# Stick-breaking attention: suffix sums on VectorE's scan instead of matmuls, and another order inside the banded-attention steps

## The reference, cut to what matters

```python
# banded: 4 key/value heads, 8 query heads each, chunks of 64 queries, keys: 16 meta + 3 chunks
m = max(max(sc), sink); e = exp(sc - m); p = e / (sum(e) + exp(sink - m))
# stick-breaking, per head of 128 columns, blocks of 128 queries
z = einsum('bhqd,bhkd->bhqk', q_blk, k) * scale
causal = key_pos[None, :] < q_pos[:, None]
log_keep = where(causal, log_sigmoid(-z), 0.0)
suffix = cumsum(log_keep, axis=3, reverse=True) - log_keep
a = where(causal, exp(log_sigmoid(z) + suffix), 0.0)
out = einsum('bhqk,bhkd->bhqd', a, v)
```

## Time and profile before

| | |
|---|---|
| median of 3 runs | 2866.44 us (2866.18 to 2867.0) |
| the profiled execution, its time | 2866.59 us |
| its span | 2864.8 us |
| PE busy | 2824.8 us (99%) |
| PE weight loads busy | 2442.3 us (85%) |
| DVE busy | 1244.1 us (43%) |
| ACT busy | 976.8 us (34%) |
| POOL busy | 1166.4 us (41%) |
| mean DMA | 86 GB/s |

### The profile page before, as it was taken

How to read it: one execution, slowest core, us unless ns; L and a number is a source line. 1 busy time by engine, 2 the same in 40 slices (tenths; PEclk the granted TensorE clock), 3 DMA queues, 4 the chain that set the end, 5 groups by cost and what they waited for, 6 DMA issues and landing times.

```text
span 2864.8 us, 41154 instructions
## 1 busy us (share of the span) xinstructions
PE 2824.8 (99%) x16928; PEld 2442.3 (85%) x16928; DVE 1244.1 (43%) x2202; ACT 976.8 (34%) x1433; POOL 1166.4 (41%) x888
## 2 busy tenths in 40 slices
PE   8999999999999999999999999999999999999997
PEld 8999999999999999777877778878778787787775
DVE  6333333433343358353434352723323244455646
ACT  4323222222323244344233344532323333234442
POOL 4333433334333435333434337434344343445442
PEclk9999999999999999999999999999999999999998
DMA  4122222222222212222222234222222222222222
GB/s 184 70 89 74 89 75 74 79 85 74 86 77 75 88 69 89 89 74 74 89 74 75 88 110 148 89 74 89 87 76 88 86 77 76 101 81 89 89 89 74
DMA packets 37084, 247.68 MB, mean 86 GB/s; under 512 B 3985, under 2 KB 4130, under 8 KB 8354
## 3 DMA queue, kind: packets, MB, share of 16 engines
q1 hardware_dynamic: 35728, 241.36, 23.7%
q10 hardware_dynamic: 1170, 3.70, 0.4%
HBM read 240.85 MB, written 4.19 MB: 86 GB/s over the span
## 4 chain that ended last, share of the span: by engine, by line
PE 90%; DVE 4%; ACT 2%; DMA 1%; DVEq 1%; POOL 1%; issue 0%; ACTq 0%; SPq 0%
PE pj L301 20%; PE pj L307 20%; PE pj L305 20%; PE pj L362 3%; PE pj L366 3%; PE pj L364 3%; PE pj L1138 2%; PE pj L1140 2%; PE pj L1139 2%; PE pa L508 1%; PE pa L545 1%; POOL wl L2273 1%; PE pa L1069 1%; DMA raw<-in_stream 1%; PE pa L1493 1%; PE pa L1475 1%
## 5 line engine op out<-in xcount | busy, mean ns | idle before, releaser
L2273 POOL TENSOR_TENSOR wl<-raw,wh 128x512 fp32r<-128x512 f32 x884 | 1166.2, 1351 | 1663.1 <-ACT wh L273 1663.0
L301 PE MATMUL pj<-xh,wh 128*128 128x264 f32 (+2 forms) x3728 | 1079.9, 336 | 3.5 <-POOL wl L2273 2.3
L307 PE MATMUL pj<-xh,wl 128*128 128x264 f32 (+2 forms) x3728 | 1047.4, 327 | 0.0
L305 PE MATMUL pj<-xl,wh 128*128 128x264 f32 (+2 forms) x3728 | 1045.6, 327 | 0.0
L273 ACT ACTIVATE wh<-raw 128x2048 fp32r<-128x2048 f32 x221 | 423.1, 1914 | 972.0 <-PE pj L307 620.7
L301 PEld LDWEIGHTS pj<-xh,wh 128*128 128x128 f32 x3728 | 632.4, 189 | 76.9 <-issue 19.8
L305 PEld LDWEIGHTS pj<-xl,wh 128*128 128x128 f32 x3728 | 631.3, 188 | 59.9 <-issue 5.3
L307 PEld LDWEIGHTS pj<-xh,wl 128*128 128x128 f32 x3728 | 631.3, 188 | 59.6
L388 DVE TENSOR_TENSOR acc<-pj,acc 128x528 f32<-128x528 f32 (+1 forms) x192 | 134.2, 700 | 126.7 <-PE pj L366 125.6
L362 PE MATMUL pj<-oh,wh 128*128 128x264 f32 (+1 forms) x640 | 180.1, 330 | 2.4 <-DVE acc L388 1.3
L366 PE MATMUL pj<-oh,wl 128*128 128x264 f32 (+1 forms) x640 | 177.7, 326 | 0.0
(11 more groups left out here) (317 smaller groups left out, 2726.9 us busy)
## 6 DMA issues: line engine op xcount, KB each, us to landing
raw<-in_stream SPq DMA_DIRECT2D x221, 1024.0 KB, 4.8
acc<-in_x SPq DMA_DIRECT2D x8, 528.0 KB, 10.1
out_y<-acc SPq DMA_DIRECT2D x8, 512.0 KB, 2.9
arena<-in_mem ACTq DMA_DIRECT2D x2, 1024.0 KB, 6.6
cst<-in_cst SPq DMA_DIRECT2D x1, 448.0 KB, 13.4
cos<-in_cos_a SPq DMA_DIRECT2D x1, 264.0 KB, 13.5
sin<-in_sin_a SPq DMA_DIRECT2D x1, 264.0 KB, 13.7
cos<-in_cos_b ACTq DMA_DIRECT2D x1, 264.0 KB, 2.6
```

What stands on the lines that cost most here:

```text
L301: pe.matmul(pj[:, pu, b, 0:m], whk, xh[:, k, a:a + m], start=(k == 0), stop=False)
L305: pe.matmul(pj[:, pu, b, 0:m], whk, xl[:, k, a:a + m], start=False, stop=False)
L307: ins = pe.matmul(pj[:, pu, b, 0:m], wlk, xh[:, k, a:a + m], start=False, stop=(k == KD - 1))
L2273: pool.tensor_tensor(wl[:, j, at], raw[:, j, at], wh[:, j, at].bitcast(F32), ALU.subtract).then_inc(s_part if c < LO_PARTS - 1 else s_lo, 1)
```

## The change

In the stick-breaking heads z is formed with queries on the partitions, in blocks of 128, 256, 384 and 512 columns (the operands of `sb_z` change places). DVE adds a large negative number above the diagonal (`mask`, four operations on PSUM). The three ACT passes stay. DVE adds max(z, 0), runs four `tensor_tensor_scan` operations over the reversed columns, one for each block, and subtracts the result from z in one operation. ACT takes the exponential; PE transposes ten 128x128 blocks of it (`sb_tr`, after `s_ae`) in place of the seven matmuls of `sb_c`; ACT copies them to SBUF (`S_eT`, the space of `S_sp`), and `sb_pv` reads that. The hook of `sb_c` at tile 2 step 12 (tile 5 step 12) goes; `sb_tr` stands at tile 3 step 2 (tile 6 step 2), `sb_pv` at tile 3 step 11 (before 10) and tile 6 step 9 (before 5), and the sums of squares one step later and four steps later.

In the banded attention each slot on PE does the scores first, then the product, then the transposes. DVE takes the maxima first, then copies the product, normalises, and only then runs `meanwhile`. ACT runs the sigmoid of a tile behind the tile's first slot, not ahead of it.

Three constant matrices go (`strict`, `neg_low`, `neg_ones`), and `cst` shrinks from 7 to 4 blocks of 128 columns.

```diff
@@ b_slot (PE): the block of chunk i is moved, unchanged, ahead of those of i-2 and i-1
+                c, n = i, B_CH * g + i
+                if c < B_CH:
+                    if n >= 1:
+                        pe.wait_ge(s_bexp, n)
+                    if c == 0:
+                        pe.wait_ge(s_bsk, g + 1)
+                        pe.wait_ge(s_bq, 4 * g + 4)
+                    at, lo, w = b_band(c)
...
                 c, n = i - 2, B_CH * g + i - 2
@@ b_slot_dve
-            c, n = i - 2, B_CH * g + i - 2
-            if 0 <= c < B_CH:
-                dve.wait_ge(s_bpv, n + 1)
-                dve.tensor_copy(B_qc[:, c, :], (bank1, bank3)[c % 2][:, 0:2 * P]).then_inc(s_bo, 1)
             c, n = i, B_CH * g + i
...
                 dve.tensor_scalar(B_nb, B_mx, -B_scale, None, ALU.mult).then_inc(s_bnb, 1)
-            if meanwhile is not None:
-                meanwhile()
+            c, n = i - 2, B_CH * g + i - 2
+            if 0 <= c < B_CH:
+                dve.wait_ge(s_bpv, n + 1)
+                dve.tensor_copy(B_qc[:, c, :], (bank1, bank3)[c % 2][:, 0:2 * P]).then_inc(s_bo, 1)
...
                 dve.sem_inc(s_bnorm, 1)
+            if meanwhile is not None:
+                meanwhile()
@@ b_act
-                if m > 0:
-                    sigmoid(act, O_B0 + 4 * g + m, SEQ)
-                for i, k in enumerate(B_POS[g]):
-                    if KD * m <= k < KD * (m + 1):
-                        b_slot_act(act, g, i)
+                slots = [i for i, k in enumerate(B_POS[g]) if KD * m <= k < KD * (m + 1)]
+                for i in slots:
+                    b_slot_act(act, g, i)
+                    if m > 0 and i == slots[0]:
+                        sigmoid(act, O_B0 + 4 * g + m, SEQ)
@@ sb_z
-                for i in (0, 1, 3, 2):
-                    w = SEQ - P * i
-                    ins = pe.matmul(pa[:, S_off[i]:S_off[i] + w], S_k[:, P * i:P * (i + 1)], S_q[:, P * i:SEQ],
-                                    start=(i != 3), stop=False, skip_group_check=True)
+                for i in range(NQ):
+                    w = P * (i + 1)
+                    ins = pe.matmul(pa[:, S_zoff[i]:S_zoff[i] + w], S_q[:, P * i:P * (i + 1)], S_k[:, 0:w],
+                                    start=True, stop=True, skip_group_check=True)
@@ sb_c -> sb_tr
-                pe.wait_ge(s_sp, n + 1)
+                pe.wait_ge(s_ae, n + 1)
                 for i in range(NQ):
-                    w = SEQ - P * i
-                    ins = pe.matmul(pa[:, S_off[i]:S_off[i] + w], neg_low, S_sp[:, S_off[i]:S_off[i] + w],
-                                    start=False, stop=(i == NQ - 1), skip_group_check=True)
-                    if i < NQ - 1:
-
-                        ins = pe.matmul(pa[:, S_off[i] + P:S_off[i] + w], neg_ones, S_behind[i], start=False,
-                                        stop=True, skip_group_check=True)
-                ins.then_inc(s_c, 1)
+                    for kb in range(i + 1):
+                        at = S_off[kb] + P * (i - kb)
+                        ins = pe.transpose(pa[:, at:at + P], S_e[:, S_zoff[i] + P * kb:S_zoff[i] + P * (kb + 1)], ident)
+                ins.then_inc(s_tr, 1)
@@ sb_pe
-            hooks = {1: {8: [sb_z(n)]}, 2: {6: [sb_vt(n)], 12: [sb_c(n)]}, 3: {10: [sb_pv(n, n)]},
-                     4: {2: [head_ss_pe(n, S_sq)], 8: [sb_z(n + 1)]}, 5: {6: [sb_vt(n + 1)], 12: [sb_c(n + 1)]},
-                     6: {5: [sb_pv(n + 1, n + 1)], 10: [head_ss_pe(n + 1, S_sq)]}}
+            hooks = {1: {8: [sb_z(n)]}, 2: {6: [sb_vt(n)]}, 3: {2: [sb_tr(n)], 11: [sb_pv(n, n)]},
+                     4: {3: [head_ss_pe(n, S_sq)], 8: [sb_z(n + 1)]}, 5: {6: [sb_vt(n + 1)]},
+                     6: {2: [sb_tr(n + 1)], 9: [sb_pv(n + 1, n + 1)], 14: [head_ss_pe(n + 1, S_sq)]}}
@@ sb_act
-                    act.wait_ge(s_z, n + a + 1)
+                    act.wait_ge(s_zm, n + a + 1)
...
+                if j in (3, 6):
+                    act.wait_ge(s_tr, n + a + 1)
+                    act.activation(S_eT, pa[:, 0:S_ZW], ACT.Copy).then_inc(s_a, 1)
@@ sb_dve: softplus and the old weights give way to
+            def mask(n):
+                dve.wait_ge(s_z, n + 1)
+                for i in range(NQ):
+                    d = pa[:, S_zoff[i] + P * i:S_zoff[i] + P * (i + 1)]
+                    dve.scalar_tensor_tensor(d, tri, NEG, d, ALU.mult, ALU.add)
+                dve.drain()
+                dve.sem_inc(s_zm, 1)
+
+            def weights(n):
                 dve.wait_ge(s_l, n + 1)
                 dve.scalar_tensor_tensor(S_sp, pa[:, 0:S_ZW], 0.0, S_e, ALU.max, ALU.add)
                 dve.drain()
                 for i in range(NQ):
...
+                    x = S_sp[:, S_zoff[i]:S_zoff[i] + P * (i + 1)][:, ::-1]
+                    dve.tensor_tensor_scan(x, x, x, 0.0, ALU.add, ALU.max)
                 dve.drain()
...
+                dve.scalar_tensor_tensor(S_e, S_sp, -1.0, pa[:, 0:S_ZW], ALU.mult, ALU.add).then_inc(s_am, 1)
```

More of the change, by code:

```diff
@@ L114, in build @@
         o_in_x = (xsh[:, KD - 2:KD, :], xsl[:, KD - 2:KD, :])
-        cst = sb("cst", 7 * P)
-        ident, ones, tri, strict, neg_low, neg_ones, tri64 = (cst[:, i * P:(i + 1) * P] for i in range(7))
+        cst = sb("cst", 4 * P)
+        ident, ones, tri, tri64 = (cst[:, i * P:(i + 1) * P] for i in range(4))
         par = sb("par", NPAR)
@@ L209, in build @@
         s_l = sem("s_l")
-        s_sp = sem("s_sp")
-        s_c = sem("s_c")
+        s_zm = sem("s_zm")
+        s_tr = sem("s_tr")
         s_am = sem("s_am")
@@ L1032, in f @@
             def f(pe):
+                c, n = i, B_CH * g + i
[6 more added lines that the diff above has]
+                    at, lo, w = b_band(c)
+                    for mp in range(2):
+                        for a in range(2):
+                            h = slice(64 * a, 64 * a + 64)
+                            ins = pe.matmul(B_sc[:, 2 * a + mp, lo:lo + w], B_qc[h, c, P * mp:P * (mp + 1)],
+                                            B_K[h, g // 2, (a + g) % 2, at:at + w], start=True, stop=True)
+                    ins.then_inc(s_bs, 1)
                 c, n = i - 2, B_CH * g + i - 2
@@ L1057, in f @@
                     ins.then_inc(s_bt, 1)
[L1058 to L1071, removed]
             return f
@@ L1465, in build @@
         S_off = [0, SEQ, SEQ + 384 + P, SEQ + 384]
-        S_behind = [S_q[:, 0:3 * P], S_k[:, 0:2 * P], S_sp[:, S_off[3]:S_off[3] + P]]
+        S_zoff = [SEQ + 384, SEQ + 384 + P, SEQ, 0]
+        S_eT = S_sp
         S_scale = float(P) ** -0.5
@@ L1486, in sb_vt, with sb_tr @@
             return f
-        def sb_c(n):
+        def sb_tr(n):
             def f(pe):
-                pe.wait_ge(s_sp, n + 1)
+                pe.wait_ge(s_ae, n + 1)
                 for i in range(NQ):
-                    w = SEQ - P * i
-                    ins = pe.matmul(pa[:, S_off[i]:S_off[i] + w], neg_low, S_sp[:, S_off[i]:S_off[i] + w],
-                                    start=False, stop=(i == NQ - 1), skip_group_check=True)
-                    if i < NQ - 1:
-                        ins = pe.matmul(pa[:, S_off[i] + P:S_off[i] + w], neg_ones, S_behind[i], start=False,
-                                        stop=True, skip_group_check=True)
-                ins.then_inc(s_c, 1)
+                    for kb in range(i + 1):
+                        at = S_off[kb] + P * (i - kb)
+                        ins = pe.transpose(pa[:, at:at + P], S_e[:, S_zoff[i] + P * kb:S_zoff[i] + P * (kb + 1)], ident)
+                ins.then_inc(s_tr, 1)
             return f
@@ L1507, in f @@
                 for i in range(NQ):
-                    ins = pe.matmul(bank[3][:, P * i:SEQ], S_vn[:, i, :], S_e[:, S_off[i]:S_off[i] + SEQ - P * i],
+                    ins = pe.matmul(bank[3][:, P * i:SEQ], S_vn[:, i, :], S_eT[:, S_off[i]:S_off[i] + SEQ - P * i],
                                     start=(i == 0), stop=(i == NQ - 1))
@@ L1555, in sb_dve @@
             dve.tensor_copy(S_on[:, :], par[:, PCOL["out_norm"]:PCOL["out_norm"] + SB_HEADS][:, bass.ds(n, 2)])
-            def softplus(n):
+            def mask(n):
[6 more added lines that the diff above has]
+            def weights(n):
                 dve.wait_ge(s_l, n + 1)
@@ L1561, in softplus @@
                 for i in range(NQ):
-                    d = S_sp[:, S_off[i]:S_off[i] + P]
-                    dve.tensor_tensor(d, d, strict, ALU.mult)
+                    x = S_sp[:, S_zoff[i]:S_zoff[i] + P * (i + 1)][:, ::-1]
+                    dve.tensor_tensor_scan(x, x, x, 0.0, ALU.add, ALU.max)
                 dve.drain()
[L1566 to L1581, removed]
+                dve.scalar_tensor_tensor(S_e, S_sp, -1.0, pa[:, 0:S_ZW], ALU.mult, ALU.add).then_inc(s_am, 1)
             def read_out(n, o):
@@ L1597, in sb_dve @@
                     head_norm_dve(dve, n, S_o[:, 0, :], S_on[:, 0:1], S_rs)
-                softplus(n + a)
+                mask(n + a)
```

(5 more changed lines are left out.)

## The result

The changed kernel takes **2847.66 us** (median of 4 runs, 2846.2 to 2849.2) against 2866.45 (median of 4 runs of the kernel before): a ratio of 0.9933, 95% interval 0.9921 to 0.9946, 18.8 us less. The profiled execution took 2847.50 us, 19.1 less than the one of before. The forecast was 2845.8, in 2842 to 2850. The sum came out near, but only because two misses in the banded part cancel.

What follows compares the result with a forecast made beforehand. The prediction took PE work plus PE's waits to bound the kernel, PE being busy for 99% of the span. From 2866.59 us it took 18.7 (stick-breaking heads) and 2.1 (banded waits): 2845.8 us, 80% range 2842 to 2850.

Steps and rivals of the forecast that it cites:

- PE work in the stick-breaking heads: Ten transposes (1.12 us) replace seven suffix-sum matmuls (3.46 us) on PE: 2.34 us less a head, 18.7 us in all.
- The scans: DVE's four scans in each stick-breaking head: 3 us, at most 3.75, hidden before PE's transposes, so free.
- 7.4 us of room: Time a stick-breaking head's scans may take on DVE before PE's transposes at tile 3 step 2 must wait.
- scans become the bound: Rival, stick-breaking heads: scans past 7.4 us delay PE eight times; at 10.0 us a head no gain; chance 0.03.
- Mask and hooks behind: Stick-breaking heads: mask operations of 1.1 us stay hidden; later copy, product and output parts cost zero, smallest slack 0.6 us.
- Banded slots, the old waits: PE's two 1.07 us waits for normalised probabilities, in g = 0 and g = 3, go: 2.1 us less.
- Banded slots, the order: PE's new block order with the same matmuls costs 0, bounds ±0.1 us for each of 32 score blocks, ±3.2 us.
- Banded slots, the gate: With the gate ahead of a slot's maxima, exponentials still precede the next scores, with 0.3 to 1.2 us of slack.
- Sum: Whole kernel: 2866.59 us less 18.7 and 2.1 gives 2845.8 us.
- Rival 4: Clock falls through the ten transposes between projections; 42 us at the 1.2 GHz level would cancel the gain; chance 0.01.

Runs made afterwards that it cites:

- e2: Kernel before with only the stick-breaking part of the change, banded functions as before: 2848.37 us, ratio 0.9937.
- e9: Changed kernel with ACT's weight rounding in tiles 2 and 5 moved behind its copy of the value transposes, so POOL works after the scans: 2848.2 us.
- e8: Changed kernel with a fifth scan in each head, over 512 columns of a scratch tile: 2855.73 us.
- e5: Kernel before with only ACT's order changed, the sigmoid behind the tile's first slot: 2864.94 us, ratio 0.9994.
- e4: Kernel before with only PE's order in the banded slots changed (scores, product, transposes): 2861.82 us, ratio 0.9983.
- e1: Changed kernel with the gate read ahead of the normalisation again at the last step of the fourth gate projection: 2840.21 us, ratio 0.9908.
- e6: Kernel before with only DVE's banded order changed (maxima first, gate of a tile's last slot behind the normalisation): 2877.01 us, ratio 1.0034.
- e7: Changed kernel with scans running forward over the columns, prefix sums in place of suffix sums: 2847.62 us.

## Why the prediction was right in its number and not in all its steps

**PE work in the stick-breaking heads: right.** 18.7 us forecast, 18.8 read from starts, 18.3 with that part alone (e2). The transposes cost 1.10 us where 1.12 stood.

**The scans: free as forecast, but by luck.** I took 3 us with 3.75 as the upper bound; they took 6.91. What was wrong is the bound. It came from L1452, a row that itself stood beside POOL's work:

```profile
1886.97 5.46 POOL L2273 TENSOR_TENSOR wl<-raw,wh 128x512 fp32r<-128x512 f32 x4 [8.06 <-ACT wh L273]
```

It took 1.50 us there and 0.75 in the pair's second head, clear of POOL. Scaling it by columns, I got a slow rate, where the rows of e9 show about 1 us added to each operation; and I did not ask what POOL would do during four scans. In the clear my 3 us was right (2.97, e9). This agrees with what the Trainium skill says of the built-in scan, half throughput (DVE: opcode table, instruction layouts, handler registers and perf-mode slots, section 6): 1280 columns in 2.97 us are 2.3 ns each, against 1.2 in L1559. The forecast of 7.4 us of room was nearly right: 6.91 left 0.2 to 0.3 (e8), so it is about 7.2. Nothing in the forecast secured that 6.91 would fit, and the rival "scans become the bound" was nearer than its 0.03 says.

**Mask and hooks behind: right.** The four mask operations took 0.89 us (1.1 forecast), and no wait for the copy or for the output parts appeared. The window of a pair is busy throughout.

**Banded slots, the old waits: right.** Both waits went. The sigmoid's new place takes 0.7 of 1.07 us (e5). The rest is put down to the later turn of the transposes, which no run shows by itself.

**Banded slots, the order: sized wrong.** The step "one such change goes as one comes: 0, bounds ±0.1" failed. It is -0.2 us a slot, outside the bounds, -5.5 in all; e4 shows it alone. The gap of 0.20 us between the last transpose and the scores was in front of me, and I assumed that a like gap would arise elsewhere. It doesn't: a projection starts 0.03 us behind the last transpose. The trace of before had this too, in the slot that has no scores:

```profile
1246.40 0.27 PE L1056 MATMUL pa<-cst,arena 128*80 128x128 f32 x1
1246.42 0.48 PE L301 MATMUL pj<-xh,wh 128*128 128x512 f32 x1
```

**Banded slots, the gate: missed.** I asked what the gate behind the normalisation would do to the next maxima, and not who waits for the gate's reading itself. It is PE, for the PSUM half, and the consumer's pace changes at the border from projections to `out4`. This cost 5.5 us by starts, and 1.55 more in the one place where the clock fell. e1 takes the stalls away, and e6 makes them with DVE's order alone.

**Sum.** -18.8 - 2.1 - 5.5 + 5.5 + 1.6 = -19.3; the profiled executions differ by -19.1. The forecast was -20.8. That the two misses have the same size is chance: with the second avoided (e1), the time is 2840.2, below my range.

**The clock.** Rival 4 said that the ten transposes might lower it. They don't: windows over the four pairs of stick-breaking heads (1845 to 2300 us) show 1.00 each. In the stages that the change touches it fell behind stalls of PE, which the prediction hadn't seen: at eight of twelve in the six kernels that have them, and at neither place in the five that don't.

## What to carry to other kernels

When an operation moves behind a wait, ask two things: who waits for its result, and who waits for the buffer that it empties. The second is easily missed where the next stage fills buffers faster than the last one: here 2.7 us an output in place of 10.9 a projection. Cost block orders by starts, not by "the same instructions": the same matmuls in another order gave 5.5 us. And a duration taken from a trace belongs to what ran beside it; look at which other engine was busy before using it as a bound, and expect to pay by the operation and not by the column.

## What the runs showed of the hardware that I had not expected

- DVE's scans and POOL's operations on the weights, both on SBUF, hold each other up: scans over 1280 columns take 6.91 us beside POOL and 2.97 apart, POOL's four operations 6.17 and 5.05 (e9). Each scan ends about its own clear time behind the POOL operation beside it. The fifth scan of 512 columns, behind POOL's work, took 1.19 us, the fourth, beside it, 2.24 (e8).
- A negative step in a scan is free (e7: within 2 ns for each form, measured beside POOL).
- After a stall of 2.5 to 2.6 us PE's granted clock fell in some cases and not in others: in one execution of the changed kernel it was 1.00 behind the stall in g = 1 and 0.78 over 7.6 us behind that in g = 2, with the same work around. Over six traces it was eight of twelve such stalls. What decides it is open.
- A projection starts 0.03 us after the start of the last transpose ahead of it; the banded scores start 0.20 us after it.
